# TensorE's loop over the MLP's middle blocks, cut at another place

## The reference

```python
D_MODEL, SEQ, DEPTH = 2048, 256, 2
D_FF = 4 * D_MODEL

for l in range(DEPTH):
    ...                        # mix of layer l: input projection, branches, output projection
    x = layer_norm(ALPHA * x + mix, ln_mix_g[l], ln_mix_b[l])
    h = jnp.square(jax.nn.relu(x @ mlp_w1[l])) @ mlp_w2[l]
    x = layer_norm(ALPHA * x + h, ln_mlp_g[l], ln_mlp_b[l])
```

## Time and profile before

| what | value |
|---|---|
| median of 3 runs | 2251.03 us (2247.06 to 2254.09) |
| the profiled execution | 2247.95 us |
| its span, first to last instruction | 2246.2 us |
| PE busy | 2218.7 us, 99% |
| PE weight loads | 2009.0 us, 89% |
| DVE busy | 1335.2 us, 59% |
| ACT busy | 1043.7 us, 46% |
| mean granted TensorE clock | 0.996 |

### The profile page before, as it was taken

How to read it: one execution, slowest core, us unless ns; L and a number is a source line. 1 busy time by engine, 2 the same in 40 slices (tenths; PEclk the granted TensorE clock), 3 DMA queues, 4 the chain that set the end, 5 groups by cost and what they waited for, 6 DMA issues and landing times.

```text
span 2246.2 us, 36599 instructions
## 1 busy us (share of the span) xinstructions
PE 2218.7 (99%) x14395; PEld 2009.0 (89%) x14395; DVE 1335.2 (59%) x1482; ACT 1043.7 (46%) x1133; POOL 36.4 (2%) x68
## 2 busy tenths in 40 slices
PE   8999999999999999999999999999999999999998
PEld 8998888798899899899889999988989988988986
DVE  4999976955544545545565555567554545454455
ACT  4555555454444444344334444444544443543542
POOL 2000000000000001000000000000000000000000
PEclk9999999999999999999999999999999999999999
DMA  7555544565566566565536656565656666556653
GB/s 243 173 160 153 183 132 146 199 229 186 199 197 216 193 197 198 198 199 193 192 122 199 186 169 170 161 219 164 216 181 194 204 219 203 188 186 204 185 197 113
DMA packets 213081, 419.17 MB, mean 187 GB/s; under 512 B 12793, under 2 KB 13361, under 8 KB 211904
## 3 DMA queue, kind: packets, MB, share of 16 engines
q1 hardware_dynamic: 210832, 406.37, 56.4%
q0 software_dynamic: 1808, 10.04, 1.3%
q10 hardware_dynamic: 288, 0.52, 0.1%
HBM read 414.79 MB, written 2.10 MB: 186 GB/s over the span
## 4 chain that ended last, share of the span: by engine, by line
PE 93%; DVE 4%; ACT 1%; DMA 1%; issue 1%; POOL 0%; DVEq 0%; SPq 0%; ACTq 0%
PE gemm L1363 15%; PE gemm L1365 15%; PE gemm L1387 15%; PE gemm L1364 15%; PE gemm L1389 15%; PE gemm L1390 15%; DVE w_lo L821 1%; PE pair L1527 1%; DVE lnp L1110 1%; PE pair L1487 1%; DMA raw<-in_ev_w_out 0%; ACT w_hi L521 0%; DVE X L856 0%; PE pair L1586 0%; PE pair L1658 0%
## 5 line engine op out<-in xcount | busy, mean ns | idle before, releaser
L1236 DVE TENSOR_TENSOR w_lo<-raw,w_hi 128x1024 fp32r<-128x1024 f32 x488 | 594.3, 1225 | 544.9 <-ACT w_hi L734 525.9
L734 ACT ACTIVATE w_hi<-raw 128x1024 fp32r<-128x1024 f32 x492 | 518.6, 1060 | 658.9 <-PE gemm L1365 376.5
L1387 PE MATMUL gemm<-x_hi,w_hi 128*128 128x256 f32 x2944 | 819.2, 278 | 3.1 <-DVE w_lo L821 2.9
L1390 PE MATMUL gemm<-x_hi,w_lo 128*128 128x256 f32 x2944 | 817.1, 278 | 0.2 <-issue 0.2
L1389 PE MATMUL gemm<-x_lo,w_hi 128*128 128x256 f32 x2944 | 817.1, 278 | 0.0
L1387 PEld LDWEIGHTS gemm<-x_hi,w_hi 128*128 128x128 f32 x2944 | 556.2, 189 | 6.2 <-issue 3.6
L1389 PEld LDWEIGHTS gemm<-x_lo,w_hi 128*128 128x128 f32 x2944 | 554.0, 188 | 0.5
L1390 PEld LDWEIGHTS gemm<-x_hi,w_lo 128*128 128x128 f32 x2944 | 553.9, 188 | 0.4 <-issue 0.4
L1363 PE MATMUL gemm<-w_hi,c_hi 128*128 128x512 f32 x1280 | 501.6, 392 | 1.1 <-DVE w_lo L821 1.0
L1365 PE MATMUL gemm<-w_hi,c_lo 128*128 128x512 f32 x1280 | 500.2, 391 | 0.0
L1364 PE MATMUL gemm<-w_lo,c_hi 128*128 128x512 f32 x1280 | 499.8, 390 | 0.0
(11 more groups left out here) (189 smaller groups left out, 942.3 us busy)
## 6 DMA issues: line engine op xcount, KB each, us to landing
raw<-in_mlp_w SPq DMA_DIRECT2D x512, 512.0 KB, 4.5
raw<-in_ev_w_in SPq DMA_DIRECT2D x96, 512.0 KB, 4.3
raw<-in_od_w_in SPq DMA_DIRECT2D x96, 512.0 KB, 3.8
raw<-in_ev_w_out SPq DMA_DIRECT2D x32, 512.0 KB, 4.0
raw<-in_od_w_out SPq DMA_DIRECT2D x32, 512.0 KB, 3.8
lnp<-in_ln_mix_g POOLq DMA_DIRECT2D x2, 1024.0 KB, 7.1
lnp<-in_ln_mix_b POOLq DMA_DIRECT2D x2, 1024.0 KB, 7.2
lnp<-in_ln_mlp_g POOLq DMA_DIRECT2D x2, 1024.0 KB, 5.0
```

The costliest lines, as they stand in the source:

```text
L734: act.activation(hi_of_chunk(s), raw[:, s % RING], ACT.Copy).then_inc(hi_ready, 1)
L1236: dve.tensor_tensor(lo_of_chunk(s), raw[:, s % RING], hi_of_chunk(s).bitcast(F32), ALU.subtract).then_inc(lo_ready, 1)
L1387: pe.matmul(acc[:, m, :], high, hi(k + c), start=begin and m % 2 == 0, stop=False, skip_group_check=True)
L1390: ins = pe.matmul(acc[:, m, :], low, hi(k + c), start=False, stop=end and m % 2 == 1, skip_group_check=True)
```

## The change

The instructions of PE stand in the same order as the loops unroll to; only the place where the loop is cut is another. `mlp_tile` is split into `hidden_tile` and `back_tile`. Block 0 is written out, and the hidden half of block 1 too. The loop's body is the back half of block b and then the hidden half of block b + 1 (`ahead=1` adds one block to the values waited for); after the loop only the back half of block 3 is written out. The loop still runs twice, and the copy of each half is the same number of matmuls as before. No other engine's program is changed.

```diff
-                def mlp_tile(b, i, first_block=False, last_block=False):
+                def hidden_tile(b, i, ahead=0):
+                    first = (ahead * 2 * NT + i) * CPT + base
+                    t = tbase + i
+                    if i < 2:
+                        pe.wait_ge(x_sum, b * NT + (PARTS * NT * (layer + 1) + FB * NT * layer + ahead * NT + i - 1))
+                    else:
+                        pe.wait_ge(relu_done, b * NT + (layer * FB * NT + ahead * NT + i - 1))
+                    for c in range(CPT):
+                        s = first + c
+                        pe.wait_ge(lo_ready, b * (2 * NT * CPT) + (s + 1))
+                        turned_chunk(turned[t % 2], X_, CK * c, s, c == 0, c == CPT - 1)
...
+                def back_tile(b, j, last_block=False):
+                    i = NT + j
                     t = tbase + i
                     acc = gemm[t % 2]
...
-                for i in range(2 * NT):
-                    mlp_tile(0, i, first_block=True)
+                tile_behind_norm(2 * layer + 1, gemm[tbase % 2], base,
+                                 lambda r: pe.wait_ge((x_sum0, x_sum)[r], PARTS * NT * (layer + 1) + FB * NT * layer - 1))
+                for i in range(1, NT):
+                    hidden_tile(0, i)
+                for j in range(NT):
+                    back_tile(0, j)
+                for i in range(NT):
+                    hidden_tile(1, i)
                 with pe.Fori(1, FB - 1) as b:
-                    for i in range(2 * NT):
-                        mlp_tile(b, i)
-                for i in range(2 * NT):
-                    mlp_tile(FB - 1, i, last_block=True)
+                    for j in range(NT):
+                        back_tile(b, j)
+                    for i in range(NT):
+                        hidden_tile(b, i, ahead=1)
+                for j in range(NT):
+                    back_tile(FB - 1, j, last_block=True)
```

More of the change, by code:

```diff
@@ L1745, in first_hidden @@
                     ins.then_inc(pair_full[0], 1)
-                def mlp_tile(b, i, first_block=False, last_block=False):
+                def hidden_tile(b, i, ahead=0):
[9 more added lines that the diff above has]
+                        turned_chunk(turned[t % 2], X_, CK * c, s, c == 0, c == CPT - 1)
+                        if type(b) is int and b + ahead == 0 and i == 1 and c == RING - 1:
+                            first_hidden()
@@ L1757, in mlp_tile @@
-                    j = (i - 2) % (2 * NT)
-                    if j < NT:
-                        pe.wait_ge(relu_done, b * NT + (layer * FB * NT + j + 1))
-                    else:
[L1761 to L1769, removed]
@@ L1771, in mlp_tile @@
-                    length = CPT if layer == DEPTH - 1 and last_block and i == 2 * NT - 1 else RING
+                    if j < 2:
+                        pe.wait_ge(relu_done, b * NT + (layer * FB * NT + j + NT - 1))
+                    else:
+                        pe.wait_ge(x_sum, b * NT + (PARTS * NT * (layer + 1) + FB * NT * layer + j - 1))
+                    length = CPT if layer == DEPTH - 1 and last_block and j == NT - 1 else RING
                     for half in range(CPT // length):
@@ L1776, in mlp_tile @@
                                 if r == 0:
-                                    if i == NT and c % 2 == 0:
+                                    if j == 0 and c % 2 == 0:
                                         pe.wait_ge(h_ready, b * NT + (layer * FB * NT + c // 2 + 1))
                                     pe.wait_ge(lo_ready, b * (2 * NT * CPT) + (s + 1))
-                                final = layer == 0 and last_block and i == 2 * NT - 1 and r == RT - 1 and c == CPT - 1
+                                final = layer == 0 and last_block and j == NT - 1 and r == RT - 1 and c == CPT - 1
                                 chunk_rows(acc, C_, r, CK * c, s, c == 0, c == CPT - 1,
                                            halfway=(lambda: row_piece(2, 0)) if final else None)
-                for i in range(2 * NT):
-                    mlp_tile(0, i, first_block=True)
-                with pe.Fori(1, FB - 1) as b:
-                    for i in range(2 * NT):
-                        mlp_tile(b, i)
-                for i in range(2 * NT):
-                    mlp_tile(FB - 1, i, last_block=True)
+                tile_behind_norm(2 * layer + 1, gemm[tbase % 2], base,
[6 more added lines that the diff above has]
+                    hidden_tile(1, i)
+                with pe.Fori(1, FB - 1) as b:
+                    for j in range(NT):
[4 more added lines that the diff above has]
+                    back_tile(FB - 1, j, last_block=True)
                 at[0], at[1] = base + MLP_SLOTS, tbase + MLP_TILES
```

## The result

The changed kernel takes 2256.87 us (median of 7 runs, 2253.24 to 2258.91). The kernel before, run beside it, takes 2248.16 (7 runs, 2245.46 to 2254.09). The ratio is 1.0034, with a 95% interval of 1.0025 to 1.0044: slower by 0.34%, or 8.7 us by the medians. The time lies inside the stated range (2245 to 2257), but the forecast was no measurable change, with a chance of 0.85, and the kernel became measurably slower, to which it gave 0.09.

A forecast was written before the change was run, and what follows sets the result against it. PE was taken to bound the kernel, busy 2218.7 of 2246.2 us. The terms, -4.4 + 4.5 = +0.1 us on 2247.95, gave 2248.0; the middle of that and 2251.1 gave 2249.5 us, range 2245 to 2257.

The forecast's parts named there:

- Term 1: Old branch place, before block 2's hidden half: halt and slow pace go, 3.6 us in layer 0, 0.85 in layer 1.
- Term 2: New branch place, before block 2's back half: PE halts 2.24 us per layer, 4.5 for both, bounds 2.0 to 2.5.
- the extra instruction: One more sequencer instruction at the head of the moved loop, taken as 0.1 us.
- rival A: New branch place: halt mostly covered or branch cheap, leaving the 4.4 us gain, 2243.6 to 2247 us; chance 0.13.
- Rival C: PE's clock falls to 0.50 after the new halt, costing 3.4 us per layer, 2256.3 us; chance 0.08.
- Term 3: Block 2's back half behind the new halt: no pace loss, 2.3 us per layer as the end of the range.
- rival B: Slow pace moves to block 2's back half and the next hidden half, 5.8 us per layer, 2261.1 us; chance 0.12.
- Term 4: Loop entry and exit: about 0.1 us per register instruction and 0.08 us on leaving, both hidden.
- The late instructions of the earlier trace: Layer 1's 0.49 us halt, 3.8 us behind the old branch, looked like late instructions and should vanish.
- rival D: Block 2's slow pace has another cause and stays, with the halt added, 2253.9 us; chance 0.09.
- Both signs of being wrong: Distance at the new branch under 1 us or over 3; slow pace in a half that no branch leads to.
- The correction from the profiled execution up to the median: Profiled execution lay 3.1 us below the median 2251.03, so the forecast took the middle of 2248.0 and 2251.1.

The follow-up runs named there:

- experiments 5 and 6: 5: kernel before plus a 2 MB copy per block, 2255.09 us; 6: changed kernel with weight chunks held back until the hidden half is done, 2251.91 us.
- `after_b`: The changed kernel traced a second time with nothing changed; 2255.28 us.
- `cut6`: The kernel before with its loop cut between the second and third back tiles, long matmuls on both sides; 2244.93 us, ratio 0.9993.
- `cut2`: The kernel before with its loop cut between the second and third hidden tiles, short matmuls on both sides; 2253.69 us, ratio 1.0029.

## Why the prediction was wrong

**Term 1 (removed, 4.4 us): right in size.** The ledger has 4.3 in before. All of block 2's hidden halves run at full pace again, but for the halt:

```profile
L1387 PE MATMUL gemm<-x_hi,w_hi x256: 276/276/279, 783.5 to 870.2; 128*128 128x256 f32 x128
L1387 PE MATMUL gemm<-x_hi,w_hi x256: 276/276/279, 1886.8 to 1973.5; 128*128 128x256 f32 x128
```

Its reason was only half right. The slow pace isn't the branch's: it also came behind halts without a branch and behind block 0's transposes, where PE doesn't halt at all. What these have in common is a break in the stream of short matmuls; all 68 hidden halves of the ledger's traces that follow a back half without a halt (0.23 to 0.24 us) have the full pace. It had been taken as a fixed cost of one place.

**Term 2 (added halt, 2.24 us per layer): the step that failed.** The halts were 2.96 and 3.42 us. Its lead of 1.9 us was right: from the branch at 868.6 to the end of the last short matmul at 870.41 + 0.11 are 1.92, and in layer 1, 1973.82 - 1971.9, again 1.92. What was wrong is "the taken branch and the restart need 4.04 us", carried over as a constant. It is 873.48 - 868.6 = 4.88 and 1977.24 - 1971.9 = 5.34, so 0.84 and 1.30 us more (0.74 and 1.20 more than the 4.14 with the extra instruction). The bounds of 2.0 to 2.5 had come from the lead and from sequencer instructions only; the branch itself had none, because two values that agreed to 0.03 us were taken as its price. Both had been measured in the same quiet moment. The argument against rival A ("the two branches measured agree") was that same error. The column that shows it, the DMA share during the branch, was in the view I used. The change put the branch where the ring is being filled, and experiments 5 and 6 show the cause from both sides: 6.5 us at a share of 0.99 with long matmuls in front, 3.5 to 3.9 at 0.03 to 0.10 with short ones. The packets say where the time went: the fetch began 0.99 and 1.20 us after the start of the branch before, and 2.14 and 2.58 us after it in the changed kernel. The Trainium skill, "Runtime: NRT & Kernel Launch", Instruction fetch mechanics, says that a taken branch out of the fetched window waits for a DMA, and the traces agree. I had cited it and not asked whether that DMA would begin as early at the new place.

**Rival C (the clock falls, chance 0.08): it happened, in each of the three traces of the changed kernel, in both layers.** Its price was put at 3.4 us per layer; it was 1.5 to 1.7 for a fall of one length and 2.9 for one of two. It was ranked too low for two reasons. The halt it was weighed with was 2.2 us, not 3.0 to 3.5. And one row of a 1.75 us halt with no fall stood as evidence for halts up to 2.2. At the edges of the MLP's halves the runs show a fall after 11 of 11 distances of 3.07 us and more, after 5 of 17 of 2.0 to 3.0, and after none under 2. Even at the forecast size it was a matter of chance.

**Term 3 (the pace behind the halt) and rival B: right and rejected.** Of layer 0's 88.9 us for the back half, 3.4 us at half the clock explain 1.7, which leaves 87.2; and the hidden halves that follow take 87.05 and 87.06 us. **Term 4 (no cost at entry and exit):** no loss beyond those of the ledger shows there. The late instructions of the earlier trace rows did vanish, as term 1 said. **Rival A** fell by term 2, **rival D** by term 1. Both signs of being wrong that the prediction names came true: the distances lie over 3 us, and in `after_b` the slow pace shows up in block 0's hidden half, to which no branch leads.

**The starting point.** The correction from the profiled execution up to the median of three runs leaned on a wish to explain 3.1 us. With 7 runs the median is 2248.16, 0.2 from the profiled execution. Without it the same sum would have given 2248.0, which is further from the 2256.87 measured.

**The sum as it was.** In the profiled executions: -4.3 + 6.4 + 4.6 = 6.7 us against -4.4 + 4.5 + 0 predicted. The span grew by 5.3, since the stretches ahead of the MLP were 1.3 us shorter. The medians differ by 8.7. Two of the 7 runs lie at 2253.2 and 2253.5, the others at 2256.1 to 2258.9; block 0's slow pace (2.1 us per layer) would make such groups, and `after_b` has it once at 2255.28. For the runs without a trace this is argued, not shown. That the time lies inside the range, and 0.6 us from rival C's 2256.3, is luck: rival C had the clock too dear (6.8 us for 4.6), the halts too short (4.5 for 6.4) and the starting point 1.3 too high.

## What to carry to other kernels

The price of a taken branch holds only for the DMA traffic around it, since its instructions come by DMA and their transfer began later here under traffic: before a loop's edge is moved, compare the DMA share of the stretch at the old place and at the new one, and the lead of the queue in time, which is longest where long instructions stand in front. A halt that looks affordable by its own length can cost the clock as well, 1.5 to 2.9 us here, so put that price into the bounds of a halt of 2 us or more. Where the code can be written out, the question doesn't arise: the version without a loop had the lowest median here, at 0.9988 of the kernel before (`cut6`, at 0.9993, isn't told apart from it).

## What the runs showed of the hardware

- A taken compare-and-branch of PE took 3.46 to 3.87 us where the DMA share during it was 0.03 to 0.10 (8 branches), 4.45 to 4.93 where it was 0.56 to 0.78 (8 branches, of the changed kernel's three traces and `cut2`), and 6.46 and 6.63 at 0.99. The last instruction packet within it began 0.93 to 1.20, 2.00 to 2.58, and 4.12 and 4.31 us after the branch did, took 0.88 to 1.44 us, and the branch ended 1.34 to 1.51 us after it.
- Behind a branch a second, smaller halt can come, marked issue: 0.49 us between starts, 3.8 us behind the edge, before, and 1.43 us, 3.0 us behind it, in `cut6`. An instruction packet ended 1.25 and 1.26 us before PE went on.
- PE has two paces for the same stream of short matmuls at full clock: 113.3 ns from start to start (87.06 us for 768) and 117.9 (90.56 us for 768), with recorded durations of 276 and 281 ns. Which one follows a break in the stream (a halt, or eight transposes without a halt) differed between executions of one program, and in one of 14 traces between its layers. It was kept until the stream ended or, in the kernel before, until another halt came. What decides between them stays open.
- After eight halts of nearly equal length (2.35 to 2.56 us between starts) the granted clock fell in 2 cases.
